# First mixer of a two-block transformer kernel: fox scores from high and low parts on two row halves, head factors spread from two parts, gate logits from one matrix

## The reference, cut to what matters

```
proj = xn @ w_in
fq, fk, fv, ff, gq, gk, gv, glr, gr = split(proj)
fq = rms_norm(fq per head, fox_q_norm_g);  fk = rms_norm(fk per head, fox_k_norm_g)
log_f = log_sigmoid(ff + fox_b_f);  c = cumsum(log_f over tokens)       # per head
s[t, u] = fq_t . fk_u / sqrt(64) + c_t - c_u   for u <= t;  p = softmax(s);  out = p @ fv
g_log = log_sigmoid(glr @ gla_w_gate2 + gla_b_gate) / 16                 # glr: 512 x 16
```

## Time and profile before

| | |
|---|---|
| median of 3 runs | 2219.72 us (2219.63 to 2221.41) |
| the profiled execution | 2224.23 us, span 2222.2 us, mean granted clock 0.994 |
| PE busy | 2184.7 us, 98% |
| DVE, ACT busy | 1141.5 us (51%), 901.5 us (41%) |

### The profile page before, as it was taken

How to read it: one execution, slowest core, us unless ns; L and a number is a source line. 1 busy time by engine, 2 the same in 40 slices (tenths; PEclk the granted TensorE clock), 3 DMA queues, 4 the chain that set the end, 5 groups by cost and what they waited for, 6 DMA issues and landing times.

```text
span 2222.2 us, 28101 instructions
## 1 busy us (share of the span) xinstructions
PE 2184.7 (98%) x11450; PEld 1788.7 (80%) x11450; DVE 1141.5 (51%) x1992; ACT 901.5 (41%) x1519; POOL 0.2 (0%) x4
## 2 busy tenths in 40 slices
PE   8999999999999999999999999999999999999998
PEld 5878888788888888888887888887777878888887
DVE  4564655353434454334346667747786454434344
ACT  5554445443323333222233466546766233222224
POOL 0000000000000000000000000000000000000000
PEclk9999999999999999999999999999999999999999
DMA  5121342132233232333323532331111223233321
GB/s 182 58 69 46 100 166 76 38 95 95 95 95 96 94 97 94 107 94 102 95 76 94 163 102 85 94 97 49 30 49 39 77 95 95 95 97 102 105 86 67
DMA packets 190033, 199.45 MB, mean 90 GB/s; under 512 B 7745, under 2 KB 185042, under 8 KB 189394
## 3 DMA queue, kind: packets, MB, share of 16 engines
q1 hardware_dynamic: 189906, 197.66, 28.2%
HBM read 188.73 MB, written 2.10 MB: 86 GB/s over the span
## 4 chain that ended last, share of the span: by engine, by line
PE 94%; DVE 2%; ACT 2%; issue 1%; DMA 0%; SPq 0%; DVEq 0%; ACTq 0%
PE lin L523 27%; PE lin L525 26%; PE lin L524 26%; PE score L726 3%; PE turned L630 3%; PE mix L740 2%; PE mix L1128 1%; PE mix L976 1%; PE score L956 1%; DVE arena L1970 0%; DMA raw<-in_w_in_dram 0%; DVE wl L1951 0%; PE turned L583 0%; ACT wh L1251 0%; PE mix L1181 0%
## 5 line engine op out<-in xcount | busy, mean ns | idle before, releaser
L523 PE MATMUL lin<-xh,wh 128*128 128x512 f32 (+1 forms) x1472 | 585.2, 398 | 3.8 <-issue 1.6
L525 PE MATMUL lin<-xh,wl 128*128 128x512 f32 (+1 forms) x1472 | 570.7, 388 | 0.0
L524 PE MATMUL lin<-xl,wh 128*128 128x512 f32 (+1 forms) x1472 | 569.9, 387 | 0.0
L523 PE MATMUL lin<-ah,wh 128*128 128x512 f32 x1040 | 406.7, 391 | 1.6 <-DVE al L1962 1.4
L525 PE MATMUL lin<-ah,wl 128*128 128x512 f32 x1040 | 404.8, 389 | 0.0
L524 PE MATMUL lin<-al,wh 128*128 128x512 f32 x1040 | 404.7, 389 | 0.0
L1951 DVE TENSOR_TENSOR wl<-raw,wh 128x2048 fp32r<-128x2048 f32 x130 | 298.0, 2292 | 190.6 <-ACT wh L1251 190.6
L1251 ACT ACTIVATE wh<-raw 128x2048 fp32r<-128x2048 f32 x130 | 247.7, 1905 | 265.3 <-PE lin L525 263.6
L523 PEld LDWEIGHTS lin<-xh,wh 128*128 128x128 f32 x1472 | 279.3, 190 | 66.3 <-issue 14.3
L525 PEld LDWEIGHTS lin<-xh,wl 128*128 128x128 f32 x1472 | 279.1, 190 | 57.4
L524 PEld LDWEIGHTS lin<-xl,wh 128*128 128x128 f32 x1472 | 279.6, 190 | 52.9 <-issue 1.2
(11 more groups left out here) (304 smaller groups left out, 2140.8 us busy)
## 6 DMA issues: line engine op xcount, KB each, us to landing
raw<-in_ffn_w_dram SPq DMA_DIRECT2D x60, 1024.0 KB, 5.2
raw<-in_w_in_dram SPq DMA_DIRECT2D x39, 1024.0 KB, 5.3
raw<-in_mlp_w_dram SPq DMA_DIRECT2D x32, 1024.0 KB, 5.5
raw<-in_xattn_wkv_dram SPq DMA_DIRECT2D x8, 1024.0 KB, 5.5
raw<-in_w_out_dram SPq DMA_DIRECT2D x8, 1024.0 KB, 5.1
arena<-arena SPq DMA_DIRECT2D x104, 64.0 KB, 2.0
raw<-in_ffn_w_dram SPq DMA_DIRECT2D x8, 768.0 KB, 4.5
raw<-in_xattn_wq_dram SPq DMA_DIRECT2D x4, 1024.0 KB, 5.2
```

The lines of the kernel that those rows point to most:

```text
L523: nc.tensor.matmul(o, w[0], x[0], start=first, stop=False)
L524: nc.tensor.matmul(o, w[0], x[1], start=False, stop=False)
L525: return nc.tensor.matmul(o, w[1], x[0], start=False, stop=last)
```

## The change

Four edits, all in the first mixer.

- Scores: each head tile is copied whole (128 rows, two heads) to `X_raw`, scaled there by DVE in one operation, then rounded by ACT to `X_hi` (fp32r) and its difference written by DVE to `X_lo` (in the place of `X_raw`). A head lies on partitions 0 to 63, its neighbour on 64 to 127. A score piece is now four fp32r matmuls for each head: high.high, high.low, low.high, and a fourth of a selector `X_sc` and the gates `X_cl` (high part on rows 0 to 7, low part on rows 32 to 39 of each half). The two heads alternate.
- Head factors: `X_rt` and `X_sel` are fp32r with 48 rows, the high part of the factors on rows 0 to 15 and the low part on rows 32 to 47; still one matmul for each spread.
- Gate logits: one float32 matmul for each half of the columns, straight from `X_l`; the two parts `G_lr` and their semaphore `gl_hi` go.
- Selector and gate rows: the sixteen row operations of DVE go; a fill of two tiles with zeros and one selector copy, two ACT copies and two differences of 8 rows come.

The diff, cut to its core:

```diff
-        X_q, X_k, X_v = A(8, T), A(8, T), A(QT, FOX)
+        X_raw = A(8, T)
+        X_lo, X_hi = Arena(att_end, arena_r)(8, T), Arena(A.at, arena_r)(8, T)
+        A(8, T)
+        X_v = A(QT, FOX)
+        X_cl, X_rt = ah[:, 4, :], ah[0:48, 5, :]
+        X_sc, X_sel = al[:, 4, :].rearrange("p (a n) -> p a n", a=4), al[0:48, 5:7, :].rearrange("p a (b n) -> p (a b) n", n=PART)
+
+        def x_at(j):
+            return 4 * (j % 4 // 2) + 2 * (j // 4) + j % 2
...
-                pe.wait_ge(gl_hi, 2)
+                pe.wait_ge(sm_z, 2)
                 pe.wait_ge(nm_rb, 1)
                 for a in range(2):
-                    for n in range(2):
-                        mm = nc.tensor.matmul(pt[a][:, :], gate2[0:16, a * PART:(a + 1) * PART], G_lr[n].bitcast(F32), start=(n == 0), stop=(n == 1))
-                    mm.then_inc(gl_g, 1)
+                    nc.tensor.matmul(pt[a][:, :], gate2[0:16, a * PART:(a + 1) * PART], X_l, start=True, stop=True).then_inc(gl_g, 1)
...
                             pe.wait_ge(hn_out, 8)
-                        causal_scores(pieces, lambda pc, a, tok: X_q[0:HALF + 8, 4 * i + 2 * pc[0] + a, tok],
-                                      lambda pc, a, nk: X_k[0:HALF + 8, 4 * i + 2 * pc[0] + a, 0:nk])
+                            pe.wait_ge(hn_lo, 4 * i + 4)
+                        for n, (pr, t, col) in enumerate(pieces):
+                            nk, tok = (t + 1) * PART, slice(t * PART, (t + 1) * PART)
+                            q, k = 4 * i + pr, 4 * i + 2 + pr
+                            for m in range(4):
+                                for a in range(2):
+                                    r = slice(a * HALF, (a + 1) * HALF)
+                                    if m == 3:
+                                        left, right = X_sc[r, 2 * i + pr, :], X_cl[r, 0:nk]
+                                    else:
+                                        left, right = (X_lo if m == 2 else X_hi)[r, q, tok], (X_lo if m == 1 else X_hi)[r, k, 0:nk]
+                                    mm = nc.tensor.matmul(ps[a][:, col:col + nk], left, right, start=m == 0, stop=m == 3)
+                                    if m == 3 and n == len(pieces) - 1:
+                                        mm.then_inc(at_s[a], 1)
...
-                for a in range(2):
-                    op = nc.scalar.activation((X_q if j < 4 else X_k)[0:HALF, 2 * (j % 4) + a, :], pl[c][a * HALF:(a + 1) * HALF, :], ACT.Copy)
-                op.then_inc(lin_freed[c], 1)
+                nc.scalar.activation(X_raw[:, x_at(j), :], pl[c][:, :], ACT.Copy).then_inc(lin_freed[c], 1)
...
-            act.wait_ge(sm_z, 2)
-            nc.scalar.activation(G_lr[0], X_l, ACT.Copy).then_inc(gl_hi, 1)
...
+            act.wait_ge(ls_v, 3)
+            nc.scalar.activation(X_cl[0:8], X_c, ACT.Copy).then_inc(ls_a, 1)
+            nc.scalar.activation(X_cl[HALF:HALF + 8], X_c, ACT.Copy).then_inc(ls_a, 1)
             act.wait_ge(hn_v, 2)
...
-            nc.scalar.activation(X_rt, po[1][0:16, :], ACT.Copy).then_inc(hn_c, 1)
+            nc.scalar.activation(X_rt[0:16], po[1][0:16, :], ACT.Copy).then_inc(hn_x, 1)
...
+            def head_high(n):
+
+                act.wait_ge(hn_out, n + 1)
+                nc.scalar.activation(X_hi[:, x_at(HEAD_TILES[n]), :], X_raw[:, x_at(HEAD_TILES[n]), :], ACT.Copy).then_inc(hn_hi, 1)
+
             for c in range(2):
+                for n in range(4):
+                    head_high(4 * c + n)
                 values(P0["fv"] + 1, c, X_v, 1)
...
-            low(G_lr[1], X_l, G_lr[0], gl_hi)
             conv(P0["fqk"] + 3)
             dve.wait_ge(ld_const, 16)
-            rows = slice(HALF, HALF + 8)
-            for n in range(8):
-                pick = cst[rows, CAT["sel"] + n:CAT["sel"] + n + 1]
-                nc.vector.tensor_scalar(X_q[rows, n, :], cst[rows, CAT["one"]:CAT["one"] + 1].to_broadcast([8, T]), pick, None, ALU.mult)
+            nc.vector.tensor_scalar(ah[:, 4:6, :], c_("chunk", T).unsqueeze(1).to_broadcast([PART, 2, T]), 0.0, None, ALU.mult).then_inc(ls_v, 1)
+            nc.vector.tensor_copy(X_sc, c_("sel", 4).unsqueeze(2).to_broadcast([PART, 4, PART]))
...
-            for n in range(8):
-                nc.vector.tensor_copy(X_k[rows, n, :], X_c)
             conv(P0["fqk"] + 5)
+            dve.wait_ge(ls_a, 5)
+            for a in range(2):
+                nc.vector.tensor_tensor(X_cl[32 + HALF * a:40 + HALF * a], X_c, X_cl[0:8].bitcast(F32), ALU.subtract)
...
+            dve.wait_ge(hn_x, 1)
+            low(X_rt[32:48], po[1][0:16, :], X_rt[0:16], hn_c)
             conv(P0["fv"] + 2)
-            for n, j in enumerate(HEAD_TILES):
+
+            def head_scaled(n):
+
+                j = HEAD_TILES[n]
+                gain = ROWS["fox_q_norm_g" if j < 4 else "fox_k_norm_g"]
+                head = X_raw[:, x_at(j), :]
                 dve.wait_ge(hn_b, n + 1)
-                for a in range(2):
-                    r = slice(a * HALF, (a + 1) * HALF)
-                    gain = ROWS["fox_q_norm_g" if j < 4 else "fox_k_norm_g"]
-                    head = (X_q if j < 4 else X_k)[0:HALF, 2 * (j % 4) + a, :]
-                    op = nc.vector.scalar_tensor_tensor(head, head, gT[0:HALF, gain:gain + 1], (ps + pt)[n % 4][r, :], ALU.mult, ALU.mult)
-                op.then_inc(hn_out, 1)
+                nc.vector.scalar_tensor_tensor(head, head, gT[:, gain:gain + 1], (ps + pt)[n % 4][:, :], ALU.mult, ALU.mult).then_inc(hn_out, 1)
+
+            def head_low(n):
+
+                at = x_at(HEAD_TILES[n])
+                dve.wait_ge(hn_hi, n + 1)
+                low(X_lo[:, at, :], X_raw[:, at, :], X_hi[:, at, :], hn_lo)
+
+            for n in range(0, 8, 2):
+                head_scaled(n)
+                head_scaled(n + 1)
+                if n:
+                    head_low(n - 2)
+                    head_low(n - 1)
+            head_low(6)
+            head_low(7)
```

More of the change, by code:

```diff
@@ L143, in constants @@
     put("sin", np.sin(ang).T[p % (HALF // 2)] * np.where(p % HALF < HALF // 2, -1.0, 1.0)[:, None])
-    sel = np.zeros((PART, 8))
-    sel[HALF + np.arange(8), np.arange(8)] = -float(HALF) ** 0.5
+    sel = np.zeros((PART, 4))
+    for pair_ in range(4):
+        for a in range(2):
+            sel[HALF * a + 2 * pair_ + a + 32 * np.arange(2), pair_] = -float(HALF) ** 0.5
     put("sel", sel)
@@ L206, in build, with __init__ @@
         AW = 16360
+        arena_at = -(-nc.sbuf_base // 32) * 32
         arena = sb("arena", [PART, AW])
+        arena_r = nc.alloc_sbuf_tensor_at("arena_r", [PART, AW], F32R, offset=arena_at)
         class Arena:
-            def __init__(self, at=0):
+            def __init__(self, at=0, store=arena):
                 self.at = at
+                self.store = store
             def __call__(self, *shape):
@@ L216, in __call__ @@
                 assert self.at + n <= AW, (self.at, n)
-                v = arena[:, self.at:self.at + n]
+                v = self.store[:, self.at:self.at + n]
                 self.at += n
@@ L257, in build @@
         hn_sq, hn_mm, hn_v, hn_std, hn_t, hn_c, hn_b, hn_out = (sem("hn_" + n) for n in ("sq", "mm", "v", "std", "t", "c", "b", "out"))
+        hn_x, hn_hi, hn_lo = sem("hn_x"), sem("hn_hi"), sem("hn_lo")
         xn_sq, xn_mm, xn_std, xn_rs, xn_out = (sem("xn_" + n) for n in ("sq", "mm", "std", "rs", "out"))
@@ L268, in build @@
         rp_a, rp_c, rp_d, rp_s = sem("rp_a"), sem("rp_c"), sem("rp_d"), sem("rp_s")
-        gl_g, gl_z, gl_y, gl_f, gl_a, gl_at, gl_i, gl_s, gl_oi, gl_on, gl_hi = (
-            sem("gl_" + n) for n in ("g", "z", "y", "f", "a", "at", "i", "s", "oi", "on", "hi"))
+        gl_g, gl_z, gl_y, gl_f, gl_a, gl_at, gl_i, gl_s, gl_oi, gl_on = (
+            sem("gl_" + n) for n in ("g", "z", "y", "f", "a", "at", "i", "s", "oi", "on"))
         ml_u, ml_hi, ml_lo, ml_s, ml_e = sem("ml_u"), sem("ml_hi"), sem("ml_lo"), sem("ml_s"), sem("ml_e")
@@ L296, in build @@
         A = Arena(1024)
-        X_rt = A(T)[0:16]
+        A(T)
         X_h1, X_h2, X_std, X_inv, X_rs = (A(QT, 16) for _ in range(5))
-        A = Arena(2048)
-        X_sel = A(8, PART)[0:16]
+        A = Arena(3072)
         H_sq = A(2, T)
@@ L317, in build @@
         G_ke = Arena(att_end)(2, T)
-        G_lr = [x[0:16, KT - 1, :] for x in (ah, al)]
         A = Arena(att_end)
@@ L2096, in _ @@
             dve.wait_ge(ld_early, 16)
-            nc.vector.tensor_copy(X_sel.rearrange("p m (a n) -> p (m a) n", a=2), ident[0:16, 0:16].unsqueeze(2).to_broadcast([16, 16, HALF]))
+            each = X_sel.rearrange("p m (a n) -> p (m a) n", a=2)
+            nc.vector.tensor_copy(each[0:32], ident[0:32, 0:16].unsqueeze(2).to_broadcast([32, 16, HALF]))
+            nc.vector.tensor_copy(each[32:48], ident[32:48, 32:48].unsqueeze(2).to_broadcast([16, 16, HALF]))
             inverse("mix")
@@ L2111, in _ @@
```

(17 more changed lines are left out.)

## The result

The changed kernel ran in 2210.1 us (median of 5, 2205.89 to 2210.29) against 2219.72 (median of 5, 2218.58 to 2221.92): ratio 0.995, 95% interval 0.9936 to 0.9965, so faster by 9.6 us and clear of the 4.4 us that can be told from none. The forecast was 2207.8 with a range of 2204 to 2214. The kernel was measured twice more beside the experiments: 2207.16 and 2206.19 us, each with a ratio of 0.9938 (intervals 0.9926 to 0.9949 and 0.9926 to 0.9951). Over all 15 runs of the changed kernel the median is 2207.75, over all 60 of the kernel before (e1 among them) 2220.1: 12.4 us less. The profiled execution took 2210.29 us, span 2208.4, mean granted clock 0.995.

The account below looks back on a forecast made before the run. The prediction took PE (TensorE) as the bound. Its terms, 1.7 + 1.7 + 5.0 + 4.4 = 12.8 us, with half the clock term 11.95, took the median from 2219.72 to 2207.8 us, range 2204 to 2214.

Parts of the forecast that it names:

- The bound: First mixer: PE is busy throughout, so a microsecond of matmul work removed there is a microsecond off the end.
- Gate logits: Gate products on PE: two float32 products instead of four, 1.91 us instead of 3.63, saving 1.72 us.
- Clock after them: Projections right behind the gate products: the half clock goes, 1.67 us in a profile, half (0.8) counted for the median.
- Head factors: Four spreads of the head factors: fp32r on 48 rows, 0.85 us each instead of 2.11, saving 5.0 us.
- crossing: PE's extra time going into narrow or row-half products and back: 0.39 us a spread, 0.40 a score block.
- rival D: Spreads and scores: fp32r products on fewer than 128 rows run at the float32 rate, giving 2237 us; chance 0.06.
- Scores: Ten score blocks: fp32r products on two row halves take 14.2 us instead of 18.6, saving 4.4 us.
- paired steps: Score blocks: two heads' products on opposite row halves run together in one fp32r product's time; 10.2 us in all.
- Rival C: Score blocks: the two row halves do not overlap in fp32r, 5.7 us more, 2217.9 us; chance 0.08.
- DVE and ACT: Scalings, copies and differences beside PE work: cost 0, bounds 0 and 3 us, with 1.3 us left before the scores.
- Rival B: Hand-over to scores or first spread comes late, ACT and DVE bound for 2 to 4 us: about 2211; chance 0.12.
- A: Rival: the clock drop stays, or later half-clock stretches come and go, up to 1.7 us each way: 2206 to 2210; chance 0.12.

Follow-up runs that it names:

- e1: The kernel before the change, run again with no edit: 2219.63 us (12 runs), ratio to before 1.0001.
- e2: The changed kernel with the gate logits again from two parts, four float32 products: 2209.36 us.
- e3: The changed kernel with the head factors again spread by float32 products of 16 rows: 2211.71 us.
- e4: The changed kernel with both heads of a pair read from rows 0 to 63, so the two sides cannot overlap: 2216.11 us (11 runs).
- e9: The changed kernel with the gate logits as one fp32r product per side on 80 rows, high and low parts stacked: 2205.4 us, ratio to before 0.9932.
- e6: The changed kernel with the four products of one head issued ahead of its neighbour's four, not in turn: 2207.45 us.

## Why the prediction was right

- **The bound.** PE's matmul time in this stretch set the end: from the start of the gate products to that of the gated stage before took 152.0 us (44.72 to 196.75), after 138.8 (45.16 to 183.93). 13.3 us went, the sum was 12.8, and no wait of PE took their place. The parts below come to 3.3 (gate products with the clock behind them), 5.0 and 4.9 us, 13.2 in all.
- **Gate logits.** 1.72 forecast, 1.72 measured.
- **Clock after them.** 1.67 forecast for the profile, and the half clock did go. It gave 1.56: the forecast took 0.32 us for the first projection product behind the gates at full clock, the kernel after has 0.43, so the eight take 2.04 and not 1.93. Counting it by half for the median looks too careful: e1 and e2 show it with the longer block as well, three profiles of three, though runs without a profile cannot be looked into. The sentence of the Trainium skill weighed there ("TensorE: Matmul & The Clock Gate", Part 1, low clock from idleness) does not cover this place: PE was busy for 3.58 of 3.58 us ahead of it in e2. For the stretch near 1178 us, which begins 0.1 us after a wait of 1.9 us has ended, the trace agrees with it, but e2, e3, e4 and e9 have that wait and no half clock there, so the wait alone is not enough.
- **Head factors.** Forecast 0.85 us a spread with its crossing, measured 0.66 + 0.32 - 0.12 = 0.86. 48 fp32r rows run at the rate of 128: the weakest assumption, rival D, is gone.
- **Scores.** Forecast 10.2 us of paired steps and 4.0 of crossings, 14.2; measured 10.1 (from e4) and 3.6, 13.7. The gain was 4.9 instead of 4.4, the difference mostly the crossings, taken from blocks between projections (0.40) where most lie between a mix and transposes. Rival C is refuted by e4.
- **DVE and ACT.** No cost, as forecast. The scalings of 128 rows followed each other every 0.66 us instead of 0.76; the slack ahead of the scores was 1.8 us instead of 1.3. Rival B did not come.
- **The first median.** 2.3 us above the forecast, and what A named fits it: later half-clock stretches come and go. In four of those five runs the mean clock was 0.995. The 15 runs give 2207.75; that this is the forecast to 0.1 us is in part luck, since the sum fell 0.5 us short of the chain (12.8 against 13.3) and the clock term stood in it by half. Why the stretch near 1178 us falls in some executions and not in others is not settled.

## What to carry to other kernels

Two products of up to 64 rows each that lie on different halves of the partitions cost PE one, in float32 and in fp32r, in turn or head by head (e6); going there and back costs some 0.4 us, so pack whole blocks. The 3.6 us of float32 products on 16 rows cost twice, in their own time and in the clock behind them; stacking high and low parts on the rows of one fp32r product brought the block to 0.47 us (e9). Where times scatter by a few us, read the chain between two fixed points, and beside it spans at equal mean clock, not medians of five; spans at equal mean clock do not show what an edit does to the clock.

## What was not expected of the hardware

- Row halves overlap whatever the order of issue: a block of one piece takes 1.14 us with the products in turn or four and four in a row, and in both its products start in pairs (e6).
- The granted clock halved behind PE work without a gap: 3.6 us of 16-row products, three profiles of three, and never with 1.91 us of them (nine profiles).
- A VectorE scaling from PSUM took 0.74 us over 128 partitions and over 64; in a row they started 0.66 us apart over 128 and 0.75 to 0.78 over 64. Why is not shown.
- The executions of one kernel scatter by 4 us with their mean clock (2204.2 us at 0.997, 2208.2 at 0.995), about as much as one of the change's three parts is worth. The stretch of 6.83 us near 1178 us is in all three profiles of the changed kernel (mean clock 0.995 each), together with others.
